# The opening of a one-core decoder step: first weight chunk in parts, two column groups side by side, a later sum of squares of x

## The reference, cut to what matters

```python
h = rmsnorm(x, g_mix)                 # x * rsqrt(mean(x*x) + eps) * g_mix
proj = h @ w_in                       # 1024 -> 2048: [pool u | q | k | v], 512 columns each
q, k = rope(q, pos), rope(k, pos)
# then: causal pooling of u, block attention of q, k, v, projection w_out with residual,
# cross attention with memory keys/values (w_ck, w_cv, w_cq, w_co), squared-relu MLP
# (w_up, w_down), final rmsnorm
```

## Time and profile before

| | us |
|---|---|
| three runs | 449.13, 450.35, 451.85 |
| median | 450.35 |
| span of the profiled execution | 447.9 |
| PE busy in it | 423.8 (95%) |
| idle time of PE, waiting for another engine, in the first 50 us | 8.0, 4.1 and 1.4 |

### The profile page before, as it was taken

The page is one execution under the profiler, slowest core; times in us unless marked ns, Lnnn a source line. Parts: engine busy times, 40 slices in busy tenths (PEclk is TensorE's granted clock), DMA queues, the critical chain, the costliest instruction groups (busy, mean ns, idle before and its releaser), DMA issues.

```text
span 447.9 us, 8424 instructions
## 1 busy us (share of the span) xinstructions
PE 423.8 (95%) x3346; PEld 393.0 (88%) x3346; DVE 266.7 (60%) x417; ACT 229.5 (51%) x411; POOL 39.1 (9%) x49
## 2 busy tenths in 40 slices
PE   2699899999999999999999999999999999999992
PEld 2699787787988999795599999999999999999992
DVE  2676787889454587654316967766666633444304
ACT  5777657664355474434026746656666533353202
POOL 0621001450000030000002200000000000020000
PEclk9979999999999999999989999999999999999998
DMA  7899897485699887597716655555555555545002
GB/s 273 286 280 343 324 265 240 161 283 170 185 352 317 334 277 284 173 368 281 266 36 246 235 190 187 189 190 189 187 187 184 186 180 176 176 168 179 1 1 97
DMA packets 42409, 96.80 MB, mean 216 GB/s; under 512 B 3954, under 2 KB 20466, under 8 KB 42234
## 3 DMA queue, kind: packets, MB, share of 16 engines
q1 hardware_dynamic: 40962, 93.03, 60.9%
q10 hardware_dynamic: 1408, 3.23, 1.9%
HBM read 91.94 MB, written 4.54 MB: 215 GB/s over the span
## 4 chain that ended last, share of the span: by engine, by line
PE 77%; ACT 8%; DVE 7%; issue 3%; DMA 2%; POOL 2%; ACTq 0%; SPq 0%; DVEq 0%; POOLq 0%
PE psum L865 68%; PE psum L666 4%; ACT w_hi L881 2%; DVE w_lo L1080 2%; DMA raw<-in_w_in 2%; POOL ssq L1306 1%; ACT swapped L881 1%; PE psum L791 1%; PE psum L778 1%; ACT soft L1024 1%; ACT act_hi L881 1%; DVE soft L1191 1%; PE psum L813 1%; DVE stats L1194 1%; PE psum L686 0%
## 5 line engine op out<-in xcount | busy, mean ns | idle before, releaser
L1080 DVE TENSOR_TENSOR w_lo<-raw,w_hi 128x1024 fp32r<-128x1024 f32 x82 | 103.1, 1268 | 90.5 <-ACT w_hi L881 90.0
L865 PE MATMUL psum<-act_hi,w_hi 128*128 128x264 f32 (+1 forms) x416 | 122.5, 294 | 9.0 <-DVE act_lo L1084 8.0
L881 ACT ACTIVATE w_hi<-raw 128x1024 fp32r<-128x1024 f32 x82 | 85.5, 1054 | 76.3 <-PE psum L865 64.2
L865 PE MATMUL psum<-act_lo,w_hi 128*128 128x264 f32 (+1 forms) x416 | 119.7, 288 | 0.0
L865 PE MATMUL psum<-act_hi,w_lo 128*128 128x264 f32 (+1 forms) x416 | 119.5, 287 | 0.0
L865 PEld LDWEIGHTS psum<-act_hi,w_hi 128*128 128x128 f32 x416 | 80.2, 193 | 12.9 <-DVE w_lo L1080 8.3
L865 PEld LDWEIGHTS psum<-act_lo,w_hi 128*128 128x128 f32 x416 | 80.0, 192 | 0.2
L865 PEld LDWEIGHTS psum<-act_hi,w_lo 128*128 128x128 f32 x416 | 79.8, 192 | 0.0
L1306 POOL TENSOR_TENSOR ssq<-ssq,sq 128x264 f32<-128x264 f32 (+1 forms) x31 | 25.4, 818 | 339.5 <-ACT sq L902 337.0
L865 PE MATMUL psum<-hid_hi,w_hi 128*128 128x264 f32 x176 | 50.1, 284 | 0.0
L865 PE MATMUL psum<-hid_lo,w_hi 128*128 128x264 f32 x176 | 50.1, 284 | 0.0
(11 more groups left out here) (155 smaller groups left out, 769.1 us busy)
## 6 DMA issues: line engine op xcount, KB each, us to landing
raw<-in_w_down SPq DMA_DIRECT2D x20, 512.0 KB, 3.3
raw<-in_w_up SPq DMA_DIRECT2D x18, 512.0 KB, 4.3
raw<-in_w_in SPq DMA_DIRECT2D x16, 512.0 KB, 5.4
raw_more<-in_w_up SPq DMA_DIRECT2D x14, 512.0 KB, 4.4
raw_more<-in_w_down SPq DMA_DIRECT2D x12, 512.0 KB, 4.2
keysT<-in_cache_k SPq DMA_DIRECT2D x16, 256.0 KB, 4.4
stage<-in_cache_v SPq DMA_DIRECT2D x16, 256.0 KB, 4.1
raw<-in_w_ck SPq DMA_DIRECT2D x8, 512.0 KB, 5.2
```

What stands on the lines that cost most here:

```text
L865: mm = pe.matmul(out, a, b, start=first and m == 0, stop=end_ and m == 2)
L881: return nc.scalar.activation(out, in_, ACT.Copy, scale=scale)
L1080: V.tensor_tensor(lo_of(c), raw_of(c), hi_of(c).bitcast(F32), ALU.subtract).then_inc(w_lo_ready, 1)
```

## The change

The opening is rewritten; everything from the third column group on stays as it is.

- The first eight chunks are taken in the order `OPENING`: chunks of q and k alternate at first (q0, k0, q1, k1, q2, q3, k2, k3). The text calls the place in the new list a position. A q chunk and a k chunk that stand side by side use the same two x tiles. The q group ends at position 5, the k group at position 7 as before.
- The first chunk is loaded, split and used in two halves of 128 rows, with waits of its own; PE takes its products pass by pass as the parts come. x tiles 0 and 1 and the gains are issued by ACT instead of SP. The load of position 3 stands ahead of those of x tiles 4 to 7.
- The job `("stat", "x")` is gone. In its place PE sums the squares behind the products of position 5, into free columns of banks 0 and 1, ACT takes the root and DVE the reciprocal at the start of their turn 5, ahead of the rotary work on q.
- ACT starts squaring after x tiles 2 and 3 are rounded, and puts the rest of x between the squares.
- At the very start PE multiplies zeros, nine times, as soon as POOL has cleared them.

```diff
@@ plan_chunks
+    chunks[:len(OPENING)] = [chunks[c] for c in OPENING]
+OPENING = (0, 4, 1, 5, 2, 3, 6, 7)
+FIRST_END = OPENING.index(3)
@@ plan_jobs
-    put(2, ("stat", "x"))
@@ SP
-            sp.dma_start(gains[:, :], ins["gains"]).then_inc(gains_landed, 16)
-            for i in range(4):
-                if i < RAW:
-                    load_weights(i)
+            def load_x(i):
                 sp.dma_start(xT[:, CK * i:CK * (i + 1), :], ins["x"][:, CK * i:CK * (i + 1), :]).then_inc(x_landed[i], 16)
+            sp.dma_start(raw_of(0)[:, 0, :], ins[w_of[w]][n, k // CK][:, 0, :]).then_inc(first_landed, 16)
+            sp.dma_start(raw_of(0)[:, 1, :], ins[w_of[w]][n, k // CK][:, 1, :]).then_inc(raw_landed[RAW_RING[0][0]], 16)
+            load_weights(1)
+            load_x(1)
+            load_weights(2)
             load_weights(RAW)
+            load_x(2)
+            load_x(3)
@@ PE
+            def warm_up():
+                pe.wait_ge(warm_ready, 1)
+                for _ in range(WARM):
+                    pe.matmul(psum[:, 7, 0:P], std[:, 0:P], std[:, 0:P], start=True, stop=True)
+            def sum_x_squares():
+                pe.wait_ge(tables_landed, 16)
+                pe.wait_ge(sq_added, KT - 1)
+                half = T // 2
+                for i in range(2):
+                    last = pe.matmul(x_sums()[:, i, :], ones, ssq[:, 0, i * half:(i + 1) * half], start=True, stop=True)
+                last.then_inc(x_sums_full, 1)
...
+                if c == FIRST_END:
+                    sum_x_squares()
@@ ACT
+            act.dma_start(xT[:, 0:CK, :], ins["x"][:, 0:CK, :]).then_inc(x_landed[0], 16)
+            act.dma_start(gains[:, :], ins["gains"]).then_inc(gains_landed, 16)
...
+            split_hi(1)
+            split_hi(2)
+            round_x(1)
+            square("x", 0, xT[:, 0, :], T)
+            square("x", 1, xT[:, 1, :], T)
+            for s in SPLITS_AT[0]:
+                split_hi(s)
+            square("x", 2, xT[:, 2, :], T)
+            square("x", 3, xT[:, 3, :], T)
+            round_x(2)
+            round_x(3)
+            for k in range(4, KT):
                 square("x", k, xT[:, k, :], T)
...
             for c in range(NC):
+                if c == FIRST_END:
+                    root_of_x()
@@ DVE
+                if c == FIRST_END:
+                    dve.wait_ge(x_root_ready, 1)
+                    V.reciprocal(rstd[:, 0, :], std[:, :]).then_inc(rstd_ready, 1)
@@ POOL
+            nc.gpsimd.memset(std[:, 0:P], 0.0).then_inc(warm_ready, 1)
```

More of the change, by code:

```diff
@@ L619, in load_weights @@
                 slot, _, prior = RAW_RING[c]
-                if prior is not None:
-                    sp.wait_ge(w_lo_ready, prior + 1)
+                if prior == 0:
+                    sp.wait_ge(first_lo_ready, CK)
+                elif prior is not None:
+                    sp.wait_ge(w_lo_ready, prior)
                 elif slot >= RAW:
@@ L837, in wait_moving, with open_first_group @@
                     pe.wait_ge(hid_lo_ready, k + CK)
+            def warm_up():
+                pe.wait_ge(warm_ready, 1)
+                for _ in range(WARM):
+                    pe.matmul(psum[:, 7, 0:P], std[:, 0:P], std[:, 0:P], start=True, stop=True)
+            def open_first_group():
+                g, w, n, k, _ = CHUNKS[0]
+                hi, lo = hi_of(0), lo_of(0)
+                banks = banks_of(g)
+                for kk in range(CK):
+                    pe.wait_ge(first_hi_ready, kk + 1)
+                    pe.wait_ge(stream_hi, kk + 1)
+                    for x, bank in enumerate(banks):
+                        pe.matmul(psum[:, bank, 0:T], hi[:, kk, x * P:(x + 1) * P], act_hi[:, k + kk, :], start=kk == 0, stop=False)
+                    pe.wait_ge(stream_lo, kk + 1)
+                    for x, bank in enumerate(banks):
+                        pe.matmul(psum[:, bank, 0:T], hi[:, kk, x * P:(x + 1) * P], act_lo[:, k + kk, :], start=False, stop=False)
+                    pe.wait_ge(first_lo_ready, kk + 1)
+                    for x, bank in enumerate(banks):
+                        mm = pe.matmul(psum[:, bank, 0:T], lo[:, kk, x * P:(x + 1) * P], act_hi[:, k + kk, :], start=False, stop=False)
+                mm.then_inc(w_used, 1)
+            def sum_x_squares():
[5 more added lines that the diff above has]
+                last.then_inc(x_sums_full, 1)
+            warm_up()
+            open_first_group()
             for c, (g, w, n, k, last_of_group) in enumerate(CHUNKS):
+                if c == 0:
+                    continue
                 hi, lo = hi_of(c), lo_of(c)
-                pe.wait_ge(w_lo_ready, c + 1)
+                pe.wait_ge(w_lo_ready, c)
                 wait_moving(c)
@@ L898, in square @@
                     act.wait_ge(sq_added, added)
[L899 to L900 removed]
+                if k == 0 and m == 2:
+                    act.wait_ge(x_sums_full, 1)
+                elif k == 0 and m > 2:
+                    wait_full(act, ("stat", {3: "m", 4: "c"}[m]))
                 dst = ssq[:, m % 2, 0:n] if k == 0 else sq[:, k % SQ_SLOTS, 0:n]
@@ L1039, in run, with round_x @@
                     own_keys(1)
-            act.wait_ge(pad_ready, 1)
-            nc.scalar.activation(cols[:, 5:6], cols[:, 4:5], ACT.Sqrt)
-            act.wait_ge(gains_landed, 16)
-            for i in range(4):
-                if i < AHEAD:
-                    split_hi(i)
+            def round_x(i):
                 act.wait_ge(x_landed[i], 16)
@@ L1256, in run, with less_x @@
                         V.tensor_tensor(dst, src, high.bitcast(F32), ALU.subtract).then_inc(free, 1)
-            dve.wait_ge(gains_landed, 16)
-            for k in range(KT):
-                if k % CK == 0 and k // CK < AHEAD:
-                    split_lo(k // CK)
+            def less_x(k):
                 dve.wait_ge(stream_hi, k + 1)
                 less(act_lo[:, k, :], xT[:, k, :], gains[:, GAIN["x"], k:k + 1], act_hi[:, k, :]).then_inc(stream_lo, 1)
+            dve.wait_ge(gains_landed, 16)
+            for k in range(CK):
+                dve.wait_ge(first_hi_ready, k + 1)
+                lo = V.tensor_tensor(lo_of(0)[:, k, :], raw_of(0)[:, k, :], hi_of(0)[:, k, :].bitcast(F32), ALU.subtract)
+                lo.then_inc(first_lo_ready, 1)
+                less_x(k)
+            split_lo(1)
+            split_lo(2)
+            less_x(2)
+            less_x(3)
             for s in SPLITS_AT[0]:
                 split_lo(s)
+            for k in range(4, KT):
+                less_x(k)
             dve.wait_ge(tables_landed, 16)
             for c in range(NC):
+                if c == FIRST_END:
+                    dve.wait_ge(x_root_ready, 1)
+                    V.reciprocal(rstd[:, 0, :], std[:, :]).then_inc(rstd_ready, 1)
                 if CHUNKS[c][4]:
```

30 lines of the change are left out of this document (21 added, 9 removed).

## The result

In thirteen runs each, on the same chip, the changed kernel took 451.72 us (median; 449.59 to 453.88) and the kernel before 449.49 us (447.64 to 453.3). The ratio is 1.0051, with a 95% interval of 1.0026 to 1.0076: the rewritten opening makes the kernel **half a per cent slower, about 2.2 us**. The forecast was 2.8 us slower.

A forecast was written before the change was run, and what follows sets the result against it. The prediction took PE, busy 423.8 of 447.9 us, as the bound, the opening being worth the shift of the first scores plus the clock behind. 1.1 + 1.7 = 2.8 on the span gave 450.7, median 453.1 us; 8-in-10 range 448.7 to 455.5.

The forecast's parts named there:

- Step 1: Splits of positions 4 to 8 on ACT: position 4's split begins at 17.8 us instead of 19.16, 1.36 us earlier.
- Step 2: Chunk 8, issued at 23.35, lands at 29.05 us; its split stands ahead of the root, which starts at 30.1, not 26.5.
- quick chunk 8: Rival: chunk 8 lands in 3.3 us, at 26.65; scores start at 46.1, 1.3 early; 450.7 or 449.0 us; chance 0.14.
- Step 3: From the root to the first scores: 18.4 us of rotary work, scores at 48.5 instead of 47.42, path 1.1 us longer.
- Step 4: Clock behind PE's stop ahead of the scores: half clock costs between 0 and 2.8 us, taken as 1.7.
- The designed gain: Rival: root starts with the sums at 26.5, scores at 44.4, 3.0 early; 449.0 us with clock loss, 447.3 without; chance 0.12.

The follow-up runs named there:

- Experiment 1: Changed kernel with the split of position 8 made in the middle of q's rotary work instead of ahead of the root; 450.58 us, ratio 1.0017 to the kernel before.
- 2: Changed kernel with the load of position 8 issued ahead of the second pair of key transfers instead of behind it; 450.43 us, ratio 1.0017 to the kernel before.
- experiment 4: Changed kernel with 38 unused products in free columns of bank 3, filling PE's stop ahead of the first scores; 450.21 us, ratio 1.0014 to the kernel before.
- experiment 9: Changed kernel with 38 unused products filling the stop ahead of the first scores, in the scores' own bank; 450.88 us, ratio 1.0017 to the kernel before.
- 11: Changed kernel with only the first scores hung on position 10 instead of 9; 451.85 us, ratio 1.0031 to the kernel before.
- 12: Kernel before the change with only the scores hung on chunk 10 instead of 9; 449.48 us, ratio 0.9982 to the kernel before.
- 7: Changed kernel with position 8's split behind the root and 34 unused products filling the stop, in the scores' bank; 449.18 us, ratio 0.9982 to the kernel before.
- 10: Changed kernel with position 8's split behind the root and the first two scores hung on position 10 instead of 9; 448.59 us, ratio 0.9959 to the kernel before.
- experiment 8: As 7, plus 8 extra products ahead of each of the later sums over partial outputs; 448.80 us, ratio 0.9979 to the kernel before.
- 3: Changed kernel without the nine zero products at the head; 450.58 us, ratio 1.0026 to the kernel before.
- 6: Changed kernel with the old order of chunks (all of q, then all of k); 450.59 us, ratio 1.0007 to the kernel before.

## Why the prediction was right

**What bounds.** The prediction said that the opening is worth the shift of the first scores and the clock behind them. That held: 1.4 us at the start, 4.1 us of wait and the half clock from 22 us (2.8 us) are all saved, and the scores don't come earlier. Most of it lies in PE's new waits ahead of them, 3.0 us for rope_a and 3.2 us more than before for kT, and in 3.4 us of half clock from 36.88 us. That it was the right size is in part luck: the shift of the scores, 1.1 us in the sum, was 0.3; the clock, 1.7 in the sum, was 1.1 by 96 us in the first profile and nearly nothing in the second; and 0.6 us came from a place that the sum put at nothing. As a median 453.1 us was forecast and 451.72 measured. Some of that gap is in the conversion: the forecast added 2.45 us to the span, and the profiled execution of the changed kernel took 1.8 us more than its span.

**Step 1** was 1.3 us too late, and this term of the sum was mis-sized: the third chunk's split began at 8.97 and not at 10.35, so position 4's split began at 16.53, not 17.8 (the chain came out 0.1 us longer than summed). Everything up to the root moved with it: chunk 8's issue 22.12 (23.35), its landing 27.66 (29.05), the root 28.66 (30.1). I had counted one issue slot (0.45 us) for it, and it was issued 0.48 us sooner, at 2.60 instead of 3.08; but its split began 1.8 us sooner. Another difference stands behind it: x tiles 4 to 7, issued from 3.55 us before, were issued only from 8.10. Whether that made it quicker was not tried. The first products, on the other hand, started at 6.60 and not at 5.3. I had counted the half split alone. It ended at 5.43; then ACT waited 0.51 us for the gains, which the change puts behind x on its queue, and rounded x (0.52 us).

**Step 2** was right in mechanism and size: 5.5 us from issue to landing against 5.7, a wait of 3.07 us, the root directly behind the split. Experiments 1 and 2 show it from two sides. The rival "quick chunk 8" fell: its split began at 27.70 and not near 26.65, and the time from issue to landing was 5.5 us and not 3.3.

**Step 3** was 0.7 too short: 19.06 us from root to scores against 18.4. The third rotary copy began 5.9 us after the root instead of 5.3, because the first rotary tile was done later. DVE waited 0.46 us for POOL's product, and that tile took DVE 0.91 us where the next took 0.43, while POOL's first two products took 1.47 beside it. From the first k copy on the forecast held exactly: 8.92 us against 8.93. The root came 1.4 us earlier than forecast and the scores 0.7 us later after the root, so the two errors partly cancel, and the shift was 0.3 us, not 1.1.

**Step 4** named the right mechanism. In the first profile the price was larger at once (2.8 us by 54 us; forecast 1.7) and smaller in the end (1.1 at 96 us, beside the 0.3 of the shift), since the slower pace of PE between 56 and 61 us in the kernel before absorbs part of it. In the second profile it was 1.5 us at the keys' attention and nothing at the memory statistic. Experiments 4 and 9 put it at 1.4 us of the mean, with 1.0 of uncertainty. The Trainium skill (TensorE: Matmul & The Clock Gate, Part 1) says that the clock is throttled by default and that activity releases it; a stop filled with products that nobody uses kept the clock at 1.00, as that says.

**What was missing from the sum** is the 0.6 us at 222 us; the second profile of the changed kernel loses as much there. The prediction added nothing behind the scores because the order of loads stays the same. The order does; the times do not, and PE comes to memory values that aren't there. **This also limits the larger gains.** From the second `softT,mv` to the last opart, PE needed 8.4 us before and 8.9 in both profiles of the changed kernel. Experiments 11 and 12 come there 1.0 us earlier than the kernel before and need 8.8 and 8.4 us, so that they keep most or all of it. Those that come 1.5 to 2.9 us earlier need more: 10.4 in 2, 9.5 in 7, 11.3 in 1 and 11.7 in 10 (8 has products of its own in this stretch). The relation is a rough one: 3, 4, 6 and 9 come there as late as the kernel before or later and need 7.9 to 9.5. Experiment 1 is 2.5 us ahead of before at the memory statistic and 0.4 behind at the last opart. In 1, 2 and 10 half clock for 3.4 us comes on top, from 219.7, 220.3 and 219.7 us, after waits of 1.0, 0.3 and 1.3 us; 4 and 7 wait 0.9 and 0.7 us there and keep the clock, so the wait alone doesn't explain it. What makes the transfers late differs. In 10 SP issued the first of the two `more_keysT` loads 2.85 us earlier than before (210.96 against 213.81), as PE was, but they took 7.6 and 8.4 us to land instead of 5.9 and 6.7. In 1 they landed in 6.1 and 6.4 us, but issuing the first took SP 2.36 us instead of 0.43, and the second was issued at 213.67. Why, stays open.

**The designed gain** of 3 us was not seen in the time of any version, though in experiment 1 the scores do start 2.5 us before those of the kernel before. With the wait for chunk 8 removed and the stop filled (7), no loss is left; with the scores moved instead (10), the kernel measures 0.4% faster than before, with the cautions given there.

The sum of the shift (0.3), the clock (1.1) and the late loss (0.6) is the 2.0 us of the profiled span. That the median moved by 2.2 in both groups while the second profile of the same kernel shows only 0.6 says that this split is that of one execution. What the repeated timings support is that removing the root's wait gives 1.3 us, filling the stop 1.4 us, and both together 2.9 us (experiments 7 and 8), each to within 1 us.

## What to carry to other kernels

When an opening is reworked, look for the first moment at which both kernels must be at the same point, and ask what ends last there; all that is won before it is worth that shift. Look at each engine's program order for an operation that needs a late transfer and stands ahead of work that is ready: a split that was harmless behind the root held it, and the scores, up by 2.8 us ahead of it. A stop of the matrix engine can have a second price behind it: stops of 2.2 us and more ahead of the scores or the transposes each went with 3.4 to 6.8 us of half clock, and those of 1.0 to 1.6 us ahead of the scores with none. So a change that gathers small waits into one long one can lose time even when the end of the wait doesn't move. Filling the stop with unused products gave it back; filling it with work that is due anyway (10) measured lowest, but is not resolved from that.

## What the runs showed of the hardware that was not expected

- **Scattered waits can lower the clock too, but need not.** In the changed kernel the clock was at half from 36.88 for 3.4 us, after PE had been busy 1.96 of 3.88 us (33 to 36.88 us), in pieces; no single wait there was over 1.2 us. Experiments 9 and 11 show the same, and the second profile of the changed kernel 6.8 us. In experiment 4 PE was busy just as little (1.96 of 3.90 us from 33 us) and the clock stayed at 1.00:

```profile
36.00:47.00 11.00, 9.30 (x75) 8.85 (x74) 7.54 (x14) 9.83 (x23) 4.79 (x6) 1.00 0.90 313
```

- **The price of the same stop varies.** The stop of 4.0 to 4.6 us was followed by 6.8 us of half clock in one execution of the changed kernel and by 3.4 in another; in experiment 1 a stop of 4.48 us was followed by 3.4. Half the stop doesn't halve the price: after 2.38 us (10) it was 3.4 us, after 2.21 (12) 6.8.
- **Half clock between 219 and 232 us**, once or twice for 3.4 us, stands in every profile but those of experiments 3 and 9, without a wait of more than 1.3 us. It begins 2 to 4 us after one of the sums over partial outputs has started, sixteen products of 4 columns that take 1.95 us; that they cause it is not shown. 8 more products of 256 columns ahead of each (experiment 8) did not prevent it.
- **Half an operation isn't half the time.** ACT's split of half a chunk took 0.63 us (`w_hi`, 512 columns) where a whole one takes 1.06.
- **A start in free columns reaches the rest of the bank.** In experiment 4 the further products wrote columns of bank 3 that v doesn't use, and v's running sum in that bank was lost: outputs that depend on v are off by up to 0.36, relative, and with the same products in another bank (experiment 9) they are right. The Trainium skill (PSUM — Partial Sum Buffer, PSUM: the matmul accumulator) says that a first product clears the accumulation state of its whole bank; the run agrees, and the edit of experiment 9, in a bank about to be overwritten, avoids it.
- **A small transfer behind a large one is late.** The gains (24 KB) were issued first by SP before and landed in 1.8 us; now ACT issues them at 1.21 us behind x, and they take 4.7 us, to 5.9. ACT waits 0.51 us for them ahead of the first rounding of x:

```profile
4.80 0.63 ACT L938 ACTIVATE w_hi<-raw 128x512 fp32r<-128x512 f32 x1 [1.63 <-DMA raw<-in_w_in]
5.94 0.52 ACT L938 ACTIVATE act_hi<-xT,gains 128x264 fp32r<-128x264 f32 x1 [0.51 <-DMA gains<-in_gains]
```
